# A two-layer block with a product-key expert layer: key stage in whole slabs, a shorter key search, and another order on ScalarE

## The chip, the core and the metric

The kernel runs on one core of one Trainium2 chip, in one launch. The metric is the device time of an execution in microseconds (us); lower is better. The core has TensorE (PE, with its weight loads as PEld), VectorE (DVE), ScalarE (ACT), GpSimd (POOL) and SyncE (SP), and 16 DMA engines that all its queues share.

## The reference, cut to what matters

Both layers end in the same expert layer, and it takes about three quarters of the time. It has 16,384 experts of 2048 numbers each, in two tables `u` and `v` (128 MB each). For each of 256 tokens and 8 heads it takes the 16 best of 128 scores in each of two halves, the 16 best of the 256 sums of those, and the experts that they name:

```python
sc = jnp.einsum('bshtd,htkd->bshtk', q, subkeys)
top_s, top_i = lax.top_k(sc, 16)
cand = top_s[..., 0, :, None] + top_s[..., 1, None, :]
best_s, best_c = lax.top_k(cand.reshape(b, s, 8, 256), 16)
i1 = take_along_axis(top_i[..., 0, :], best_c // 16)
i2 = take_along_axis(top_i[..., 1, :], best_c % 16)
idx = i1 * 128 + i2;  gate = softmax(best_s)
hid = einsum('td,tkd->tk', x, u[idx])
out = einsum('tk,tkd->td', gelu(hid) * gate, v[idx])
```

## The kernel before

**Two ways to the same rows.** For 192 of the 256 tokens (`ND`) the kernel multiplies with all experts: `u` is read as 128 slabs of 128 experts (1 MB each), and gates, zero nearly everywhere, pick the chosen ones. For the first 64 tokens (`NS`) it gathers the chosen rows: 64 gathers a layer (`PAIRS`, 1 MB each, 128 rows), each followed by a dot of the 128 rows with the tokens' x. The gathers stand on GpSimd's queue and land in two buffers (`SLOTS`); gather n+2 waits for dot n.

**A slab of `u`.** SyncE's queue loads the slab into `raw` (three buffers, `RAW_SLABS`). A slab has two halves of 128 x 1024 (pieces); a ring of four (`RING`) holds their rounded-up part `wh`, made by ScalarE (`hi`, L597), and their rest in half precision, `halves`, made by VectorE (`lo`, L1743), which needs `wh` and frees `raw`. TensorE (`slab_u`, L1073) does for each half eight high products (`ps <- xx,wh`, 384 columns: the sum of the high part of x and the side sum with its low part) and eight side products (`ps <- halves`, 192 columns); all matmuls share L1043. ScalarE copies the side sums of a slab to `cross` (`take_side`, L637); after the first half of the next slab TensorE adds them by a product with the identity (`fold`); then ScalarE takes the result out through gelu (`gelu`, L777), to `arena` in the key stage or `hring` in the spread stage, from where SyncE stores it.

**Order.** Each engine runs what is written out for it; semaphores join them. ScalarE's order in each slab stands in `trip`: side sums, high half, gelu, high half. VectorE's order is a table: `UNIT_FILL` says how many low halves (`L`) and dots (`D`) stand in each of seven gaps of a unit of the search.

**The stages of the expert layer.** The key stage is slabs 0 to 63, in trips of four. Beside it VectorE searches in 16 units (8 heads, two blocks of 128 tokens): `max` finds eight values, `max_index` their places, `match_replace` takes them out; two halves of 128 scores, then 256 sums, then compares and sums that look the indices up (L1973 to L1993). The tail of a unit is decoded within the next unit. Unit 8 ends with the row indices (`idx_f`), which TensorE spreads over partitions ahead of slab 20 (`REP_TRIP` 5), and then the gathers can start. After unit 16 come softmax and selection, and TensorE turns them ahead of slab 64. The spread stage is slabs 64 to 127, in eight trips of eight. In each, six groups (`Q_PIECE`) of four tokens get their dense gates: VectorE compares (`compare`, L2051, two instructions), ScalarE scales eight rows (`gate_rows`, L792, to `hot_w`), TensorE multiplies them, ScalarE copies the gates out (`gates_out`, L783), VectorE multiplies the kept slabs (`gate_kept`, L2043). Here dots stand after the halves of `DOT_PIECE`, 46 in eight trips. Then `v` is multiplied (the V stage), in which the rows of `v` are gathered too.

## Time and profile before

| what | value |
|---|---|
| median of 3 runs | 3280.0 us (3279.31 to 3281.93) |
| profiled execution: its own time | 3274.78 us |
| its span, mean granted clock | 3273.0 us, 0.996 |
| busy share: PE, PEld, DVE, ACT, POOL | 98%, 84%, 85%, 61%, 12% |
| moved by DMA | 969 MB, mean 296 GB/s |

| stage | layer 0 | layer 1 |
|---|---|---|
| key stage, slabs 0 to 63 | 511 to 811 us | 2056 to 2356 us |
| spread stage, slabs 64 to 127 | 811 to 1131 us | 2356 to 2675 us |
| PE, DVE, ACT busy in the key stage | 287.4, 289.2, 173.6 us | 286.0, 288.5, 173.1 us |
| PE, DVE, ACT busy in the spread stage | 309.3, 298.2, 283.9 us | 310.3, 298.7, 284.4 us |

Busy shares are means over stages; the stages are read apart. A slab is told by its fold, a matmul from `cross` that occurs once a slab. A timeline row gives start, duration, operation and count of instructions put together, and in brackets what the engine waited for just before. A wait is put down to what came last.

### The profile page before, as it was taken

To read this page: it belongs to the slowest core of one execution; us is meant where nothing else is said; L and a number is where in the kernel's file an instruction comes from. 1 tells how busy PE (TensorE), PEld (TensorE's weight loads), DVE (VectorE), ACT (ScalarE), POOL (GpSimd) and SP (SyncE) were. 2 spreads that over 40 slices of the span, in tenths; PEclk is the share of its full clock that TensorE was granted. 3 is DMA by queue.
4 is the path that set the end of the run, shared out by engine and by line. 5 is a ranking of instruction groups with operands and counts; after the bars stand their busy time and mean duration, and the time that the engine had idled before them with its cause. 6 is when DMAs were issued, how large, how long until landed. Compare 5 with 4: busy or idle time off the path is not lost. (4 is left out here: it accounts for less than half of the span.)

```text
span 3273.0 us, 52190 instructions
## 1 busy us (share of the span) xinstructions
PE 3196.3 (98%) x19468; PEld 2762.0 (84%) x19468; DVE 2773.5 (85%) x4026; ACT 1997.0 (61%) x3631; POOL 406.6 (12%) x266
## 2 busy tenths in 40 slices
PE   9999999999999999999999999999999999999998
PEld 8888888889888888888888887888888888888887
DVE  5775669999999888888887756999999988888887
ACT  4444556556898755555555545655688875555555
POOL 0000000011111122222100000001111112222220
PEclk9999999999999999999999999999999999999999
DMA  7553345698999989999984344578899999999995
GB/s 273 183 183 140 116 161 192 257 342 339 379 379 378 373 335 372 362 371 367 365 305 156 117 152 158 197 278 338 335 390 380 373 369 366 368 370 368 363 368 224
DMA packets 169221, 969.07 MB, mean 296 GB/s; under 512 B 18912, under 2 KB 52704, under 8 KB 55648
## 3 DMA queue, kind: packets, MB, share of 16 engines
q1 hardware_dynamic: 132192, 698.61, 56.2%
q0 software_dynamic: 36864, 268.45, 22.3%
q8 instruction: 80, 1.31, 0.1%
q14 instruction: 85, 0.70, 0.1%
HBM read 951.26 MB, written 15.73 MB: 295 GB/s over the span
## 5 line engine op out<-in xcount | busy, mean ns | idle before, releaser
L597 ACT ACTIVATE wh<-raw 128x1024 fp32r<-128x1024 f32 x1264 | 1335.5, 1060 | 833.5 <-PE ps L1043 663.9
L1043 PE MATMUL ps<-xx,wh 128*128 128x384 f32 (+1 forms) x5504 | 1333.7, 358 | 6.8 <-DVE xx L1755 4.0
L1043 PE MATMUL ps<-wh,act 128*128 128x512 f32 x3584 | 1190.6, 390 | 0.4 <-issue 0.2
L1746 DVE TENSOR_TENSOR wl<-raw,wh 128x1024 fp32r<-128x1024 f32 x752 | 905.9, 1221 | 323.8 <-ACT wh L597 322.2
L1043 PEld LDWEIGHTS ps<-xx,wh 128*128 128x128 f32 x5504 | 955.5, 189 | 73.5 <-issue 5.7
L1043 PE MATMUL ps<-wl,act 128*128 128x512 f32 x2304 | 897.6, 390 | 0.0
L1043 PEld LDWEIGHTS ps<-wh,act 128*128 128x128 f32 x3584 | 673.8, 188 | 142.0 <-DVE wl L1746 1.0
L1743 DVE SCALAR_TENSOR_TENSOR halves<-raw,wh 128x1024 f16<-128x1024 f32 x512 | 615.2, 1213 | 63.5 <-ACT wh L597 63.1
L1043 PEld LDWEIGHTS ps<-wl,act 128*128 128x128 f32 x2304 | 433.2, 188 | 89.7
L1043 PE MATMUL ps<-halves 128*128 128x192 f16 x4096 | 428.3, 248 | 22.5 <-DVE halves L1743 20.6
L1043 PEld LDWEIGHTS ps<-halves 128*128 128x128 f16 x4096 | 312.7, 98 | 112.4 <-issue 62.8
L1043 PE MATMUL ps<-xx,wl 128*128 128x256 f32 x1408 | 393.9, 280 | 0.0
L1711 POOL DMA_INDIRECT arena<-in_urows,idx x128 | 150.9, 1179 | 1907.3 <-DVE idx L2018 1072.0
L1711 POOL DMA_INDIRECT arena<-in_v,idx x128 | 246.8, 1928 | 839.4 <-DVE arena L2126 818.4
L2126 DVE SCALAR_TENSOR_TENSOR arena<-arena,hid 128x2048 f32<-128x2048 f32 x128 | 300.2, 2345 | 2.2 <-DMA arena<-in_v,idx 2.1
L1928 DVE SCALAR_TENSOR_TENSOR arena<-arena 128x2048 f32<-128x2048 f32 x128 | 292.0, 2281 | 0.0
L1043 PEld LDWEIGHTS ps<-xx,wl 128*128 128x128 f32 x1408 | 266.2, 189 | 0.5
L792 ACT ACTIVATE hot_w<-hot,x_space 128x128 f16<-128x128 f16 x768 | 242.1, 410 | 8.0 <-DVE hot L2051 8.0
L637 ACT ACTIVATE cross<-ps 128x192 fp32r<-128x192 f32 (+1 forms) x272 | 89.8, 330 | 124.5 <-PE ps L1043 122.2
L1043 PE MATMUL ps<-cross,ident_r 128*128 128x192 f32 (+1 forms) x272 | 92.0, 338 | 16.9 <-ACT cross L637 15.7
L777 ACT ACTIVATE arena<-ps 128x192 f32<-128x192 f32 x128 | 42.1, 329 | 108.3 <-PE ps L1043 108.2
L1043 PE MATMUL ps<-arena 64*128 64x128 f32 (+9 forms) x712 | 93.3, 317 | 7.5 <-DVE arena L2004 4.6
(225 smaller groups left out, 1751.2 us busy)
## 6 DMA issues: line engine op xcount, KB each, us to landing
raw<-in_u SPq DMA_DIRECT2D x256, 1024.0 KB, 7.1
raw<-in_v SPq DMA_DIRECT2D x256, 1024.0 KB, 7.4
raw<-in_w SPq DMA_DIRECT2D x118, 1024.0 KB, 4.8
h_scratch<-hring SPq DMA_DIRECT2D x128, 96.0 KB, 7.3
hring<-h_scratch SPq DMA_DIRECT2D x128, 96.0 KB, 7.1
arena<-in_memT SPq DMA_DIRECT2D x4, 512.0 KB, 7.2
raw<-in_w SPq DMA_DIRECT2D x4, 512.0 KB, 7.8
arena<-in_xT SPq DMA_DIRECT2D x4, 512.0 KB, 8.5
```

The source lines that it names most:

```text
L597: nc.scalar.activation(wh[:, j, :], raw_piece(p), ACT.Copy, scale=W_UP if scaled_up(p) else 1.0)\
L637: nc.scalar.activation(cross[:, 0:n], ps[:, bank, n:2 * n], ACT.Copy).then_inc(cross_out, 1)
L777: nc.scalar.activation(h_kept[:, k, :] if kept else hring[:, j, :], ps[:, j, 0:ND], ACT.Gelu, scale=W_DOWN).then_inc(evac_done, 1)
L792: nc.scalar.activation(hot_w[:, q % 2, w, t, :], one_hot(q, 0, t), ACT.Copy, scale=gate_hl[w][:, of // NS, of % NS:of % NS + 1]).then_inc( ...
L1043: return nc.tensor.matmul(out, lhs, rhs, start=start, stop=stop, **kw)
L1711: pool.indirect_dma_start(out=gbuf[n % SLOTS], out_offset=None, in_=rows_of, in_offset=bass.IndirectOffsetOnAxis(ap=idx[:, j:j + 1], axis=0))\
L1743: v.scalar_tensor_tensor(out=wl16[:, j, :], in0=raw_piece(p), scalar=W_UP, in1=wh[:, j, :].bitcast(F32), op0=ALU.mult, op1=ALU.subtract).t ...
L1746: v.tensor_tensor(wl[:, j, :], raw_piece(p), wh[:, j, :].bitcast(F32), ALU.subtract).then_inc(lo_ready, 1)
L1928: v.scalar_tensor_tensor(out=rows_u, in0=rows_u, scalar=1.0, in1=xrep, op0=ALU.mult, op1=ALU.mult, accum_out=hid[:, j:j + 1]).then_inc(slo ...
L2126: v.scalar_tensor_tensor(out=vacc, in0=rows_v, scalar=hid[:, j:j + 1], in1=vacc, op0=ALU.mult, op1=ALU.add).then_inc(slot_free, 1)
```

## The change

- **TensorE.** `slab_u` does a slab in one go: 16 high products (the fold of the slab before after the tenth, `FOLD_AT`), then 16 side products. It waits for both high halves, then for both low halves.
- **High and low halves.** One instruction makes both halves of a slab (`hi_slab`, `low_slab`, 128 x 2048). On ScalarE the order in a slab becomes side sums, high halves, gelu, and in the spread stage gates out and gate rows.
- **Search.** Two units run interleaved, in eight steps; each works on its scores in place (no copy), and on 112 sums and not 256: the first 4 of one half with all 16, the other 12 with the first 4. Decoding is done for four units at once (`batch`, nine steps) in half precision, the steps standing between those of the next pair.
- **Placing.** The search ends by slab 42 (`EXP_SLAB`), the row indices are spread ahead of slab 12, the selection is turned ahead of slab 48 (`SEL_TRIP` 12). Ten dots stand in the last pairs and the last batch, and then one after each low slab up to slab 63 (22 and four around the softmax); the spread stage has four a trip, after every second slab.
- **Gates.** `compare` is one instruction for both one-hot halves; its constant `iota_h` moves from x's free space to free space in `halves`, and is set up at slab 51. The 16 chunks of x in half precision lie in four parts of five (`XS`).

Cut to its core (removed lines that the kernel above shows are left out):

```diff
+XS = 5
...
-REP_TRIP = 5
+REP_TRIP, SEL_TRIP = 3, 12
...
+FOLD_AT = 9
...
-UNIT_FILL = ([("L", "", "L", "", "L", "L", "")] * 2 + [("L", "L", "L", "", "L", "L", "")]
-             + [("L", "L", "L", "L", "L", "L", "")] * 7 + [("LL", "LL", "LL", "LL", "LDL", "LL", "DL")]
-             + [("LDLL", "", "LDLL", "L", "LDLL", "L", "L")] * 4 + [("LDLL", "", "LLL", "L", "LDLL", "L", "L")])
-UNIT_TAIL = ("L", "LD", "L", "L", "L", "", "")
-SPARED = (2, 5)
+PAIR_FILL = ([("L", "", "L", "", "L", "", "L", "")] * 3
+             + [("S", "S", "", "S", "S", "", "S", "S"), ("S", "S", "S", "S", "S", "", "S", "S"),
+                ("S", "S", "D", "S", "S", "SD", "S", "S"), ("S", "S", "SD", "S", "S", "SD", "S", "S"),
+                ("S", "S", "D", "S", "S", "SD", "S", "S")])
+LAST_FILL = ("S", "D", "S", "D", "S", "D", "S", "D", "S")
+BATCH = 4
+KEY_PAIRS = 4 * TOPK + (TOPK - 4) * 4
+EXP_SLAB, SETUP_SLAB, REST_DOTS = 42, 51, 22
+DOT_SLABS = (1, 3, 5, 7)
...
+    iota_h = halves[:, RING - 1, PC + ND:PC + ND + 4 * P]
...
+        def hi_slab(p):
+
+            act.wait_ge(piece_used, p - (RING - 1))
+            act.wait_ge(lo_ready, p - 2)
+            n, j = p // 2, p % RING
+            act.wait_ge(raw_full[n % RAW_SLABS], 16 * (n // RAW_SLABS + 1))
+            nc.scalar.activation(wh[:, j:j + 2, :], raw[:, n % RAW_SLABS, :].rearrange("p (e c) -> p e c", e=2), ACT.Copy,
+                                 scale=W_UP if scaled_up(p) else 1.0).then_inc(hi_ready, 2)
...
-                    ahead = [2 * s + 2, 2 * s + 3]
                     take_side(u0, i * slabs + (s - 1), (s - 1) % 2, ND)
-                    for n in ahead[:-1]:
-                        hi(i * (2 * slabs) + (u0 + n), n % RING)
                     if first and s == 1:
                         scores_out(layer, PEER_H - 1)
+                    hi_slab(u0 + 2 * (i * slabs + s + 1))
                     gelu(i * slabs + (s - 1), s - 1)
-                    for n in ahead[-1:]:
-                        hi(i * (2 * slabs) + (u0 + n), n % RING)
                     for k in range(Q_TRIP) if spread else ():
...
+            for i in range(1, SEL_TRIP):
+                trip(i, BODY, exp_at=EXP_SLAB % BODY if i == EXP_SLAB // BODY else None)
...
+            j = 2 * s4 % RING
+
+            def part(w, kc):
+                return w[:, j + kc // (KC // 2), kc % (KC // 2) * P:(kc % (KC // 2) + 1) * P]
+
+            pe.wait_ge(hi_ready, piece + 2)
+            for kc in range(KC):
+                last = mm(both, part(wh, kc), xx[:, kc, :, NS:], kc == 0, False, skip_group_check=True)
+                if kc == FOLD_AT and side_of is not None:
                     fold(side_of, 1 - par_, side_t0)
-                if then is not None:
-                    then(e)
+            last.then_inc(piece_used, 1)
+            if then is not None:
+                then(0)
+            pe.wait_ge(lo_ready, piece + 2)
+            for kc in range(KC):
+                if x_from is not None and kc % XS == 0:
+                    pe.wait_ge(x16_ready, x_from + kc // XS + 1)
+                last = mm(side, part(wl16, kc), x16[:, kc // XS, kc % XS, :], False, kc == KC - 1, skip_group_check=True)
+            last.then_inc(piece_used, 1)
+            if then is not None:
+                then(1)
...
+            def low_slab():
+                n = next(at_slab)
+                p = u0 + 2 * n
+                j = p % RING
+                dve.wait_ge(hi_ready, p + 2)
+                dve.wait_ge(piece_used, p - 2)
+                v.scalar_tensor_tensor(out=wl16[:, j:j + 2, :],
+                                       in0=raw[:, p // 2 % RAW_SLABS, :].rearrange("p (e c) -> p e c", e=2), scalar=W_UP,
+                                       in1=wh[:, j:j + 2, :].bitcast(F32), op0=ALU.mult, op1=ALU.subtract)\
+                    .then_inc(lo_ready, 2)
...
+            def unit(i, step):
+                keys, b = sc[:, i, :, :], i % 2
+                tv, ti, rest = top_v[:, b, :, :], top_i[:, b, :, :], s1[:, b, :, :]
+                sums, left = cand[:, b, 0, :], cand[:, b, 1, :]
+                values = sel[:, 2, i * TOPK:(i + 1) * TOPK]
+                found = best_i[:, i // BATCH % 2, 0, i % BATCH * TOPK:(i % BATCH + 1) * TOPK]
+                if step == 0:
+                    if i < PEER_H:
+                        dve.wait_ge(sc_evac, PEER_H * layer + i + 1)
+                else:
+                    own.upto(marked[i])
+                if step == 0:
+                    for t in range(2):
+                        own.mark(v.max(tv[:, t, 0:8], keys[:, t, :]))
+                elif step == 1:
+                    for t in range(2):
+                        own.mark(v.max_index(ti[:, t, 0:8], tv[:, t, 0:8], keys[:, t, :]))
+                        own.mark(v.match_replace(out=rest[:, t, :], in_to_replace=tv[:, t, 0:8],
+                                                 in_values=keys[:, t, :], imm_value=NEG))
+                elif step == 2:
+                    for t in range(2):
+                        own.mark(v.max(tv[:, t, 8:16], rest[:, t, :]))
+                elif step == 3:
+                    own.mark(v.tensor_tensor(sums[:, 0:4 * TOPK].rearrange("p (a b) -> p a b", a=4),
+                                             tv[:, 0, 0:4].unsqueeze(2).broadcast_to([P, 4, TOPK]),
+                                             tv[:, 1, :].unsqueeze(1).broadcast_to([P, 4, TOPK]), ALU.add))
+                    own.mark(v.tensor_tensor(sums[:, 4 * TOPK:].rearrange("p (a b) -> p a b", b=4),
+                                             tv[:, 0, 4:TOPK].unsqueeze(2).broadcast_to([P, TOPK - 4, 4]),
+                                             tv[:, 1, 0:4].unsqueeze(1).broadcast_to([P, TOPK - 4, 4]), ALU.add))
+                    for t in range(2):
+                        own.mark(v.max_index(ti[:, t, 8:16], tv[:, t, 8:16], rest[:, t, :]))
+                elif step == 4:
+                    own.mark(v.max(values[:, 0:8], sums))
+                    own.mark(v.tensor_copy(top_f[:, i // BATCH % 2, :, :, i % BATCH], ti))
+                elif step == 5:
+                    own.mark(v.max_index(found[:, 0:8], values[:, 0:8], sums))
+                    own.mark(v.match_replace(out=left, in_to_replace=values[:, 0:8], in_values=sums, imm_value=NEG))
+                elif step == 6:
+                    own.mark(v.max(values[:, 8:16], left))
+                else:
+                    own.mark(v.max_index(found[:, 8:16], values[:, 8:16], left))
+                marked[i] = own.n
+            def batch(b, step):
+                at, row, col = (best_i[:, b % 2, k, :] for k in range(3))
+                whole, by16, by4 = (place[:, k] for k in range(3))
+                r1, r2 = rank[:, 0], rank[:, 1]
+                tall, least = row_at[:, 0], row_at[:, 1]
+                own.upto(marked["batch"] if step else max(marked[i] for i in range(b * BATCH, (b + 1) * BATCH)))
+                if step == 0:
+                    own.mark(v.tensor_scalar(row, at, 4, None, ALU.logical_shift_right))
+                    own.mark(v.tensor_scalar(col, at, 2, None, ALU.logical_shift_right))
+                elif step == 1:
+                    own.mark(v.tensor_copy(place, best_i[:, b % 2].rearrange("p w (u k) -> p w k u", u=BATCH)))
...
+                elif step == 6:
+                    own.mark(v.tensor_tensor(pick.rearrange("p w k a u -> p (w k) a u"),
+                                             rank.rearrange("p w k u -> p (w k) u").unsqueeze(2)
+                                             .broadcast_to([P, 2 * TOPK, TOPK, BATCH]),
+                                             iota_u.unsqueeze(1).broadcast_to([P, 2 * TOPK, TOPK, BATCH]), ALU.is_equal))
+                elif step == 7:
+                    flat = pick.rearrange("p w k a u -> p w k (a u)")
+                    own.mark(v.tensor_tensor(flat, flat, top_f[:, b % 2].rearrange("p w a u -> p w (a u)").unsqueeze(2)
+                                             .broadcast_to([P, 2, TOPK, TOPK * BATCH]), ALU.mult))
+                else:
+                    for w in range(2):
+                        own.mark(v.tensor_reduce(
+                            sel[:, w, b * BATCH * TOPK:(b + 1) * BATCH * TOPK].rearrange("p (u k) -> p k u", u=BATCH),
+                            pick[:, w].rearrange("p k a u -> p k u a"), AX.X, ALU.add))
+                marked["batch"] = own.n
...
+            for p in range(UNITS // 2):
+                tail = itertools.count() if p and p % 2 == 0 else None
+                for n in range(8):
+                    for i in (2 * p, 2 * p + 1):
+                        unit(i, n)
+                        if tail is not None:
+                            step = next(tail)
+                            if step < 9:
+                                batch(p // 2 - 1, step)
+                            elif p == PEER_H // 2 and step == 10:
+                                own.upto(marked["batch"])
+                                v.scalar_tensor_tensor(out=idx_f, in0=sel[:, 0, 0:P], scalar=float(KEYS),
+                                                       in1=sel[:, 1, 0:P], op0=ALU.mult, op1=ALU.add).then_inc(sidx_ready, 1)
+                    fill(PAIR_FILL[p][n])
...
+            for n in range(9):
+                batch(UNITS // BATCH - 1, n)
+                fill(LAST_FILL[n])
...
+            for n in range(EXP_SLAB + 4, KEPT):
...
+                fill("SD")
...
+                v.tensor_tensor(hot[:, q % 2, :, :].rearrange("p w (j t) -> p w j t", t=4),
+                                iota_h.rearrange("p (j t) -> p j t", t=4).unsqueeze(1).broadcast_to([P, 2, P, 4]),
+                                sel_t[:, :, 4 * q:4 * q + 4].unsqueeze(2).broadcast_to([P, 2, P, 4]),
+                                ALU.is_equal).then_inc(onehot_ready, 2)
...
+                for n in range(WIDE):
+                    q = i * Q_TRIP + COMPARE_SLAB.index(n) if n in COMPARE_SLAB else None
+                    if q is not None:
+                        compare(q)
+                    low_slab()
+                    if q is not None and q >= 3:
+                        gate_kept(q - 3)
+                    if n in DOT_SLABS:
+                        dot()
```

VectorE where the low halves go over from the query weights (`wl`) to `u` (`halves`), layer 0. The names are buffers: `arena` holds all of the search, `raw` a slab as loaded, `wh` its high halves, `wl` and `halves` low halves. Before:

```order
L1983 TENSOR_TENSOR arena<-arena 128x512
L1986 TENSOR_TENSOR arena<-arena 128x256
L1989 MAX_INDEX arena<-arena 128x8 x2
L1746 TENSOR_TENSOR wl<-raw,wh 128x1024
L1993 TENSOR_REDUCE arena<-arena 128x2x16
L1995 MAX arena<-arena 128x8
L1746 TENSOR_TENSOR wl<-raw,wh 128x1024
L1999 CAST arena<-arena 128x32
L2000 MAX_INDEX arena<-arena 128x8
L2001 MATCH_REPLACE arena<-arena 128x256
L2007 MAX arena<-arena 128x8
```

and now:

```order
L2030 TENSOR_SCALAR arena<-arena 128x64
L1991 MAX arena<-arena 128x8 x2
L2032 CAST arena<-arena 128x192
L1768 SCALAR_TENSOR_TENSOR halves<-raw,wh 128x1024
L1994 MAX_INDEX arena<-arena 128x8
L1995 MATCH_REPLACE arena<-arena 128x128
L1994 MAX_INDEX arena<-arena 128x8
L1995 MATCH_REPLACE arena<-arena 128x128
L2034 SCALAR_TENSOR_TENSOR arena<-arena 128x64
L1994 MAX_INDEX arena<-arena 128x8
L1995 MATCH_REPLACE arena<-arena 128x128
```

What stood as one unit's steps with low halves between has become steps of two units and of a batch, in which a low half stands after several searches.

VectorE around the softmax over the selection. Before:

```order
L1928 SCALAR_TENSOR_TENSOR arena,hid<-arena 128x2048
L2027 TENSOR_REDUCE arena<-arena 128x16
L1743 SCALAR_TENSOR_TENSOR halves<-raw,wh 128x1024
L2031 TENSOR_SCALAR arena<-arena 128x16
L2032 RECIPROCAL arena<-arena 128x16
L1743 SCALAR_TENSOR_TENSOR halves<-raw,wh 128x1024
L2035 TENSOR_TENSOR arena<-arena 128x256
L1743 SCALAR_TENSOR_TENSOR halves<-raw,wh 128x1024 x2
L2063 CAST x_space<-iota 128x4x128
```

and now:

```order
L2087 COPY arena<-arena 128x16
L2088 TENSOR_TENSOR arena<-arena 128x256
L1945 SCALAR_TENSOR_TENSOR halves<-raw,wh 128x2x1024
L1963 SCALAR_TENSOR_TENSOR arena,hid<-arena 128x2048
L1945 SCALAR_TENSOR_TENSOR halves<-raw,wh 128x2x1024
L1963 SCALAR_TENSOR_TENSOR arena,hid<-arena 128x2048
L2092 TENSOR_REDUCE arena<-arena 128x16
L1945 SCALAR_TENSOR_TENSOR halves<-raw,wh 128x2x1024
L1963 SCALAR_TENSOR_TENSOR arena,hid<-arena 128x2048
L2095 TENSOR_SCALAR arena<-arena 128x16
```

Each whole slab (128x2x1024) is now followed by a dot (to `hid`), where low halves stood with one dot in eight.

ScalarE in the spread stage (`cross` side sums, `hring` gelu out, `hot_w` gate rows). Before:

```order
L597 ACTIVATE wh<-raw 128x1024
L777 ACTIVATE hring<-ps 128x192
L597 ACTIVATE wh<-raw 128x1024
L783 ACTIVATE arena<-ps 128x64x4
L637 ACTIVATE cross<-ps 128x192
L597 ACTIVATE wh<-raw 128x1024
L777 ACTIVATE hring<-ps 128x192
L597 ACTIVATE wh<-raw 128x1024
L783 ACTIVATE arena<-ps 128x64x4
L792 ACTIVATE hot_w<-hot,x_space 128x128 x8
L637 ACTIVATE cross<-ps 128x192
```

and now:

```order
L624 ACTIVATE wh<-raw 128x2048
L800 ACTIVATE hring<-ps 128x192
L806 ACTIVATE arena<-ps 128x64x4
L815 ACTIVATE hot_w<-hot,x_space 128x128 x8
L660 ACTIVATE cross<-ps 128x192
L624 ACTIVATE wh<-raw 128x2048
L800 ACTIVATE hring<-ps 128x192
L806 ACTIVATE arena<-ps 128x64x4
L660 ACTIVATE cross<-ps 128x192
L624 ACTIVATE wh<-raw 128x2048
L800 ACTIVATE hring<-ps 128x192
```

The second high half has moved ahead of the gelu, into one instruction with the first.

## Rows read from the trace of the kernel before

**Rows 1.** Stage windows; from:to, us, then busy (x instructions), PEclk, DMA share, GB/s
```profile
511.00:811.00 300.00, 287.42 (x2200) 262.35 (x2200) 289.21 (x651) 173.60 (x268) 31.93 (x20) 0.99 0.78 290
811.00:1131.00 320.00, 309.33 (x2511) 281.25 (x2509) 298.18 (x368) 283.93 (x691) 47.03 (x47) 1.00 0.97 379
1150.00:1700.00 550.00, 550.00 (x2427) 455.05 (x2426) 479.27 (x491) 307.94 (x486) 122.54 (x62) 1.00 0.94 359
...
980.00:990.00 10.00, 10.00 (x87) 9.28 (x85) 8.51 (x10) 9.70 (x25) 0.94 (x1) 1.00 1.02 418
```

**Rows 2.** TensorE timeline, layer 0; start us, us, engine line op, operands [idle before]
```profile
512.05 1.68 PE L1043 MATMUL ps<-xx,wh 128*128 128x384 f32 x8
...
690.21 0.34 PE L1043 MATMUL ps<-cross,ident_r 128*128 128x192 f32 x1
...
804.12 0.34 PE L1043 MATMUL ps<-cross,ident_r 128*128 128x192 f32 x1
804.29 1.58 PE L1043 MATMUL ps<-xx,wh 128*128 128x384 f32 x8
805.71 0.83 PE L1043 MATMUL ps<-halves 128*128 128x192 f16 x8
...
807.81 0.83 PE L1043 MATMUL ps<-halves 128*128 128x192 f16 x8
808.43 0.34 PE L1043 MATMUL ps<-cross,ident_r 128*128 128x192 f32 x1
...
811.49 1.64 PE L1043 MATMUL ps<-xx,wh 128*128 128x384 f32 x8
...
1130.12 0.36 PE L1043 MATMUL ps<-cross,ident_r 128*128 128x192 f32 x1 [0.26 <-ACT cross L637]
```

**Rows 3.** Waits, first 511 to 811 us, then 811 to 1131: us in total, times, longest
```profile
PE ps L1043 <- DVE halves L1743: 9.4, 14, 1.1
...
ACT wh L597 <- DMA raw<-in_u: 15.4, 17, 3.2
...
PE ps L1043 <- ACT cross L637: 8.5, 14, 1.5
```

**Rows 4.** TensorE timeline where the row indices are first needed
```profile
609.00 0.49 PE L1043 MATMUL ps<-arena 128*128 128x128 f32 x2 [2.29 <-DVE arena L2004]
609.29 2.85 PE L1043 MATMUL ps<-xx,wh 128*128 128x384 f32 x8
```

**Rows 5.** VectorE timeline over one unit of the search with its fills
```profile
738.42 0.29 DVE L1949 COPY arena<-arena 128x256 f32<-128x256 f32 x1
...
740.16 2.29 DVE L1928 SCALAR_TENSOR_TENSOR arena<-arena 128x2048 f32<-128x2048 f32 x1
...
742.37 2.36 DVE L1743 SCALAR_TENSOR_TENSOR halves<-raw,wh 128x1024 f16<-128x1024 f32 x2
...
765.93 0.29 DVE L1949 COPY arena<-arena 128x256 f32<-128x256 f32 x1
```

**Rows 6.** VectorE groups by form, 500 to 1130 us: x count | busy us, mean ns
```profile
L2051 DVE TENSOR_TENSOR hot<-x_space,sel_t 128x512 f16<-128x512 f16 x96 | 37.9, 434 | 0.0
...
L1973 DVE TENSOR_TENSOR arena<-arena,iota 128x512 f32<-128x512 f32 x15 | 10.3, 684 | 0.0
...
L1967 DVE FIND_INDEX8 arena<-arena 128x8 uint32<-128x128 f32 x28 | 8.0, 285 | 0.0
```

**Rows 7.** ScalarE timeline: the scores of head 5 go to SBUF
```profile
506.86 0.59 ACT L757 ACTIVATE arena<-ps 128x512 f32<-128x512 f32 x1
```

**Rows 8.** DMA issues, 660 to 800 us: count, median us from issue to landing
```profile
arena<-in_urows,idx POOLq DMA_INDIRECT x15, 8.2
```

**Rows 9.** ScalarE timeline in the spread stage: one half, gates out, eight gate rows
```profile
1092.49 1.05 ACT L597 ACTIVATE wh<-raw 128x1024 fp32r<-128x1024 f32 x1
1093.44 0.37 ACT L783 ACTIVATE arena<-ps 128x256 f32<-128x256 f32 x1
1093.70 2.52 ACT L792 ACTIVATE hot_w<-hot,x_space 128x128 f16<-128x128 f16 x8
```

204 lines of the change are left out of this document (68 added, 136 removed).

## The prediction

> **What bounds the kernel now.** I read the busy times by stage first [rows 1]. Two stages of each layer are touched: the first 64 slabs of the expert product (called the key stage here, 511 to 811 us) and the last 64 (the spread stage, 811 to 1131 us); layer 1 repeats both within 1 us in length. In the key stage TensorE is busy 287 of 300 us and VectorE 289: two engines near full. In the spread stage TensorE has 309 of 320, VectorE 298, ScalarE 284, and the DMA engines a share of 0.97 at 379 GB/s. In the V product TensorE is busy throughout, so nothing can be won there. Next, TensorE's own rows [rows 2]: from fold to fold an unhindered slab takes 808.43 - 804.12 = 4.31 us. Sixty-four of them are 276 us, while slab 0 starts at 512.05 and slab 64 at 811.49, 299.4 us later [rows 2]. The waits [rows 3] say who is late: VectorE's low halves in the key stage (9.4 us), the side sums copied by ScalarE in the spread stage (8.5 us), besides one wait of 2.29 us for the row indices [rows 4]. Behind that one the next eight matmuls took 2.85 us against 1.57 to 1.58 us elsewhere [rows 2, 4]: TensorE had idled and ran a while at 1.2 GHz, worth some 1.7 us with its side products; layer 1 shows the same wait without that slowdown. So the gain to be had is VectorE time, ScalarE order and bytes, and I follow TensorE's path through three stretches of layer 0.
>
> **Part 1: slabs 0 to 36.** VectorE's search cost now: from one unit's first instruction (738.42) to the next (765.93) are 27.5 us [rows 5]. In it are 12 low halves and 3 dots. A dot holds the engine 742.37 - 740.16 = 2.21 us, a low half about 1.13 (2.36 for two less the overlap) [rows 5], together 20.2, so a unit costs 7.3 us, 117 for 16. After the change a unit sheds its copy, sums 112 candidates and not 256, and does its index decoding in batches of four. By the kinds' durations (a search of 128 elements 285 ns [rows 6], the others by their length) I count 4.1 us for a unit (two maxima 0.5, four searches of 128 1.05, two maxima 0.4, sums 0.25, two searches 0.55, and 1.3 in the second round at half length). A batch compares and multiplies 2048 half-precision elements and reduces twice 1024. 512 such elements took 434 ns, against 684 ns in fp32 [rows 6], which puts 2048 at 1.2 us if the broadcast keeps that speed and 2.2 if not; I take 1.2, since the row before has the same inner four. The reduce I price at the fp32 rate, 2.3 in all. A batch is then 5.5 us, and the search 16 x 4.1 + 4 x 5.5 = 88 us (bounds 85 to 96), some 29 less. A low half of a whole slab should take about a dot's time, 2.2 for 2.26.
>
> Where does it go? The search is packed into 42 slabs instead of 60, and three places come late. (a) The units' pairs wait for the scores of the later one. ScalarE writes those of head 5 at 506.86 [rows 7]; pair 2 then needs 8.2 us of search, batch 0 (5.5, newly here) and four low halves (4.5), so the last half of slab 1 is done near 524.4 and TensorE ends slab 1 at 525.7, where two unhindered slabs from 512.05 on would end at 520.7 [rows 2]: 5.0 lost, some 3.6 of it new. (b) The indices come after low halves 8 to 12, batch 1 and unit 8's sixth step, at about 576. TensorE is at slab 12 by 572: it loses 4.5 us, against 2.5 now, and one slow spell (1.7) as now. (c) Pair 6 has 8.2 + 5.5 + 8 x 2.2 + 2 x 2.21 = 35.7 us for 8 slabs, 1.3 above TensorE's 34.4; with its uneven batch steps 1.9 lost. All other stretches give VectorE 3.6 to 4.2 us a slab, and it can be late by 3.0 us, the length of the 16 high products that now stand first.
>
> TensorE's slab itself gets shorter. It changes from fp32 to half-precision products and back twice a slab now, once afterwards. Eight high products behind the fold take 805.71 - 804.29 = 1.42 us; behind side products they take 2.10 less 0.62, 1.48 [rows 2], so a change back costs some 0.06. One of two goes, and the fold then stands among products of its own kind: I take 0.05 (0 to 0.1), a slab of 4.25. Sum: slab 37 starts at 525.7 + 8.5 + 3.8 (turning x, unchanged) + 34.0 + 4.5 + 25 x 4.25 + 1.9 + 1.7 = 686.4. Now it starts 2.1 us before the fold of 690.21 [rows 2], at 688.1. **Part 1: -1.7** (bounds -6 to +5).
>
> **Part 2: slabs 37 to 63.** Here 26 dots stand one behind each slab's low half, where now there are about one for two slabs. VectorE would need 2.2 + 2.21 = 4.4 us a slab, only just too much. But each slab then moves 1.05 MB of weights and 1.05 MB of gathered rows. The spread stage moves 379 GB/s at a share of 0.97 [rows 1]: nearly full. 2.10 MB at that rate are 5.5 us, at 418, a best ten-microsecond stretch [rows 1], 5.0. The gathers say the same. Two buffers: gather n+2 starts when dot n ends, and lands 8.2 us later [rows 8]; with the dot itself a pair of slabs takes at least 8.2 + 0.3 + 2.2 = 10.7, so 5.4 a slab. I take 5.4. The first gathers lie ready, so 24 intervals count: 24 x 5.4 + 4.5 = 134, from the first dot 5.2 us into the stretch; full weight buffers and VectorE's 3.0 us give back 6; one more slab follows: 134 + 5.2 - 6 + 4.7 = 137.9. The six turns of the selection (now between slabs 63 and 64) hide in it. Now the stretch takes 811.49 - 688.1 = 123.4. **Part 2: +14.5** (7 with a cycle of 5.1, 21 with 5.65).
> The Trainium skill ("DMA: Bandwidth & Descriptors", Specifications) gives a core about 358 GB/s from HBM. The row's 379 is above that, so the trace disagrees. By 358 the cycle would be an estimated 5.86 us and the stretch 11 longer a layer.
>
> **Part 3: the spread stage.** Eight slabs with six gate groups are a round. Now eight rounds take 1130.12 - 811.49 = 318.6 us [rows 2], 39.8 each; without waits it would be 8 x 4.31 + 6 x 0.5 = 37.4. Two causes. First a loop on ScalarE: fold, copy-out, second high half, gates out, eight gate rows, side copy, fold. A half takes 0.95, gates out 0.26, the rows 2.52 less the overlap of 0.1 [rows 9], and with 0.36 for the fold, 0.22 for the copy-out and 0.3 for the side sums the loop is 4.5 us, above a slab's 4.31. The change puts both halves ahead of the copy-out, so this loop loses 0.95. Second, weights that land late: ScalarE waits 15.4 us for them [rows 3] at a DMA share of 0.97. Dots fall from 5.75 to 4 a round: (12 x 1.05 + 0.8) MB in 37 us are 362 GB/s, the V stage's load (359, share 0.94), where TensorE is never kept waiting [rows 1]. ScalarE's own work is 8 x 2.29 + 6 x (0.26 + 2.42) = 34.4 us a round [rows 9], counting 1.87 for a whole slab's high half, and fits beside TensorE's 8 x 4.25 + 6 x 0.48 = 36.9, but with 2.5 us to spare only; within three slabs with gates it falls 0.9 behind, and the fold gives it 1.6. So I add 0.6 a round for late weights: 37.5, 300 in all. VectorE needs 32.5 a round. **Part 3: -18** (-22 to -6).
>
> Layer 0: -1.7 + 14.5 - 18 = -5. Layer 1 has no slow spell, and its stretches are otherwise within 1.5 us of these (the table of stages): -5 again. The profiled execution took 3274.8 us (span 3273.0 and 1.8 around it), 5.2 below the median of 3280.0; I carry the difference over: 3270.
>
> **The rivals.** *ScalarE becomes the bound of the spread stage (slower).* If late weights hit it for over 2.5 us a round, each us more is TensorE's. For: it has 93% to do, waits 2 us a round today, and everything stands in one order behind a high half that is now twice as long. Against: fewer bytes. With today's 2 us a round straight on TensorE's 36.9, rounds of 39.0 give 7 and not 18 a layer: 3292. *The run of dots is not held by bytes.* Then VectorE sets 4.4 a slab, part 2 takes 121 and saves 2: 3270 - 34 = 3236. For: gathers never made a dot wait yet; against: [rows 1, 8]. *The lower HBM rate,* worked as this kernel's mechanism: if gathers and weights together get a tenth less than the mixed traffic now, the cycle is 5.85, +11 a layer: 3292; the skill's figure above would make it so.
>
> **How the numbers follow.** My case has 0.63, its own range 3256 to 3284. ScalarE 0.17, no byte limit 0.12, lower rate 0.08. Below 3273.4 (0.2%, about what a measurement can tell from no change) lie six tenths of my case and the second rival: 0.50. Above 3286.6 lie the other two and a little of mine: 0.27. Between them 0.23. The range 3250 to 3296 leaves out the second rival and the far ends of the others.
>
> **What would show it.** Right: fold to fold 4.25 in calm slabs; a wait of 4 us in slab 1 and at the indices; from slab 38 to 63 dots 5.2 to 5.6 us apart, VectorE waiting for gathers and DMA share 1.0; the spread stage near 300 us with hardly a wait for side sums. Wrong: dots 4.4 apart, or ScalarE over 95% busy in the spread stage with folds waiting, or a low half of a slab that costs more than 2.3 us.

## The result, and the profile after

The changed kernel takes a median of 3311.95 us (3306.2 to 3312.97, four runs) against 3279.65 (3277.07 to 3281.93, four runs): a ratio of 1.0095, with a 95% interval of 1.0078 to 1.0113. It is slower by about 1%, where 3270 us was predicted and a range of 3250 to 3296. The profiled execution took 3306.2 us against 3274.78, its span 3304.0 against 3273.0.

Where the 31.0 us of span come from, by the folds (the product that closes a slab, one in each):

| stretch, fold to fold | layer 0: before, after | layer 1: before, after |
|---|---|---|
| slab 0 to 36 | 170.3, 174.2 | 169.7, 171.8 |
| slab 36 to 63 | 123.4, 155.9 | 124.3, 155.4 |
| slab 63 to 127 | 316.5, 299.5 | 315.2, 298.6 |

That is +19.4 and +16.6 us. From the last fold of layer 0 to the first of layer 1 the changed kernel is 5.1 us shorter, which the prediction has as nothing. Spread stage: -17 us a layer, as predicted (-18). First part: +3.9 and +2.1 where -1.7 was predicted. The run of dots: +32.5 and +31.1 where +14.5 was predicted, and this decides.

These are the stages of layer 0 in the windows view of the changed kernel (columns as in [rows 1]): the first slabs, the start of the run of dots, the rest of it, the spread stage.

```profile
512.00:694.00 182.00, 172.69 (x1316) 164.26 (x1315) 158.66 (x398) 95.16 (x123) 9.50 (x8) 0.96 0.71 259
694.00:760.00 66.00, 58.08 (x414) 54.67 (x412) 55.71 (x48) 33.50 (x44) 21.45 (x11) 0.95 0.90 339
760.00:850.00 90.00, 68.21 (x487) 63.67 (x488) 67.84 (x49) 34.66 (x44) 38.26 (x15) 0.96 0.87 342
850.00:1150.00 300.00, 297.30 (x2491) 285.62 (x2490) 260.85 (x228) 274.67 (x623) 50.67 (x34) 1.00 0.96 361
```

From 760 to 850 us TensorE is busy 68.2 of 90 us and VectorE 67.8: neither is the bound. GpSimd, which only issues gathers there, is busy 38.3 us, 2.6 a gather. And the DMA engines have a share of 0.87 at 342 GB/s, below the 0.97 and 379 of [rows 1]. The waits view of 694 to 850 us of the changed kernel names the chain (us in total, times, longest):

```profile
DVE arena L1963 <- DMA arena<-in_urows,idx: 32.4, 18, 3.1
...
PE ps L1063 <- DVE halves L1945: 29.6, 16, 3.1
```

VectorE waits for gathers in its dots, TensorE for the low half that stands behind each dot. One period of it, in the timeline of GpSimd and VectorE of the changed kernel:

```profile
806.84 2.29 DVE L1963 SCALAR_TENSOR_TENSOR arena<-arena 128x2048 f32<-128x2048 f32 x1 [1.57 <-DMA arena<-in_urows,idx]
809.05 0.08 DVE L1963 DVE_READ_ACCUMULATOR arena<-arena 128x1 f32 x1
809.05 2.29 DVE L1945 SCALAR_TENSOR_TENSOR halves<-raw,wh 128x2048 f16<-128x2048 f32 x1
809.41 2.74 POOL L1736 DMA_INDIRECT arena<-in_urows,idx  x1 [3.33 <-DVE arena L1963]
812.53 2.29 DVE L1963 SCALAR_TENSOR_TENSOR arena<-arena 128x2048 f32<-128x2048 f32 x1 [1.19 <-DMA arena<-in_urows,idx]
...
818.69 2.29 DVE L1963 SCALAR_TENSOR_TENSOR arena<-arena 128x2048 f32<-128x2048 f32 x1 [1.65 <-DMA arena<-in_urows,idx]
```

The dot that began at 806.84 frees its buffer; the gather into it is issued at 809.41 and its data are used at 818.69, 9.3 us later, by the next dot but one. Two dots thus take 11.85 us: 5.9 a slab. Fifteen intervals from 757.25 to 847.77 have a mean of 6.0. The issue itself takes 2.74 us. Where it begins as the low half begins, and behind another instruction, it takes 0.94 (same kernel and view):

```profile
741.90 0.42 DVE L2099 TENSOR_TENSOR arena<-arena 128x256 f32<-128x256 f32 x1
742.23 2.33 DVE L1945 SCALAR_TENSOR_TENSOR halves<-raw,wh 128x2048 f16<-128x2048 f32 x1
742.25 0.94 POOL L1736 DMA_INDIRECT arena<-in_urows,idx  x1 [5.20 <-DVE arena L1963]
```

Of the 17 issues from 747 to 846 us, 16 began within a low half (L1945), took 2.43 to 2.75 us and ended 0.8 us behind it; that is the pattern of a lock which VectorE holds for an instruction. In the kernel before a low half has half the length (the 2.35 us below are two of them), and such issues took 1.68 us:

```profile
731.64 2.35 DVE L1743 SCALAR_TENSOR_TENSOR halves<-raw,wh 128x1024 f16<-128x1024 f32 x2
731.99 1.68 POOL L1711 DMA_INDIRECT arena<-in_urows,idx  x1 [7.52 <-DVE arena L1928]
```

VectorE waited for gathers alone from 693 to 850 us, 32.4 us in 18 waits, and never for TensorE.

### The profile page after: what moved, and what is told of

Read it like the earlier page. It is cut to its first block, busy times and chain, and to the rows that moved or that the text cites. A ratio compares the mean times of both kernels' runs of the same rounds, so it can differ in the third digit from the quotient of the medians.

```text
span 3304.0 us, 51665 instructions
## 1 busy us (share of the span) xinstructions
PE 3190.4 (97%) x19468; PEld 2807.7 (85%) x19468; DVE 2691.8 (81%) x3546; ACT 1958.8 (59%) x3377; POOL 483.1 (15%) x266
## 4 chain that ended last, share of the span: by engine, by line
PE 81%; DVE 7%; DMA 7%; ACT 2%; issue 2%; SPq 0%; ACTq 0%; DVEq 0%
PE ps L1063 81%; DMA arena<-in_urows,idx 5%; DVE halves L1945 2%; DMA raw<-in_w 1%; DVE arena L1963 1%; ACT wh L624 1%; DVE wl L1771 1%; DVE arena L2054 1%; DVE xx L1780 0%; DMA arena<-in_v,idx 0%; DMA raw<-in_v 0%; DVE arena L2187 0%; DVE halves L1768 0%; ACT arena L693 0%; ACT wh L610 0%
## 5 line engine op out<-in xcount | busy, mean ns | idle before, releaser
L610 ACT ACTIVATE wh<-raw 128x1024 fp32r<-128x1024 f32 x756 | 798.7, 1062 | 771.8 <-PE ps L1063 653.4
L1063 PEld LDWEIGHTS ps<-xx,wh 128*128 128x128 f32 x5504 | 973.1, 191 | 72.9 <-issue 6.1
L1945 DVE SCALAR_TENSOR_TENSOR halves<-raw,wh 128x2048 f16<-128x2048 f32 x252 | 576.9, 2289 | 118.3 <-issue 105.8
L1736 POOL DMA_INDIRECT arena<-in_urows,idx x128 | 227.8, 1779 | 1851.3 <-DVE idx L2080 1004.7
L624 ACT ACTIVATE wh<-raw 128x2048 fp32r<-128x2048 f32 x254 | 486.2, 1914 | 13.0 <-DMA raw<-in_u 9.9
L1063 PE MATMUL ps<-halves 128*128 128x192 f16 x4096 | 388.4, 249 | 75.0 <-DVE halves L1945 66.7
L1063 PEld LDWEIGHTS ps<-halves 128*128 128x128 f16 x4096 | 332.3, 99 | 115.8 <-DVE halves L1945 82.2
L1063 PEld LDWEIGHTS ps<-arena 128*64 128x64 f32 (+4 forms) x712 | 62.4, 162 | 34.1 <-issue 16.5
```

The lines of the kernel that those rows point to most:

```text
L610: nc.scalar.activation(wh[:, j, :], raw_piece(p), ACT.Copy, scale=W_UP if scaled_up(p) else 1.0)\
L624: nc.scalar.activation(wh[:, j:j + 2, :], raw[:, n % RAW_SLABS, :].rearrange("p (e c) -> p e c", e=2), ACT.Copy, scale=W_UP if scaled_up(p ...
L1063: return nc.tensor.matmul(out, lhs, rhs, start=start, stop=stop, **kw)
L1736: pool.indirect_dma_start(out=gbuf[n % SLOTS], out_offset=None, in_=rows_of, in_offset=bass.IndirectOffsetOnAxis(ap=idx[:, j:j + 1], axis=0))\
L1945: v.scalar_tensor_tensor(out=wl16[:, j:j + 2, :], in0=raw[:, p // 2 % RAW_SLABS, :].rearrange("p (e c) -> p e c", e=2), scalar=W_UP, in1=w ...
```

## The experiments

All stretches are read from fold to fold, as in the table above; a pair of numbers is layer 0 and layer 1.

**Is it the lock?** Edit of e1_gap:

```diff
                         dot()
+                        if gap:
+                            ...
+                            own.mark(v.tensor_reduce(gap_out, xrep[:, 0:384].rearrange("p (a b) -> p a b", a=24),
+                                                     AX.X, ALU.add))
```

> The changed kernel with a small reduce (128x384) on VectorE behind each of the 26 dots of slabs 42 to 63, ahead of the next low half; its result is used by nobody. Theory lock: in the changed kernel's trace the issue of a gather on GpSimd takes 2.75 us where it begins while a whole-slab low half runs on VectorE, and ends 0.8 us after it, but 0.94 us where a reduce or cast runs. So the issue should fall to 0.94, a pair of slabs lose 1.8 us, the dots stand 5.0 to 5.2 us apart and not 5.9, slabs 37 to 63 take about 140 us and not 156, and the whole about 3280 us. Theory bytes (that of the prediction, with its rate set too high): the issue gets shorter, but the gathers land as late as now since 2.1 MB a slab are moving anyway; dots stay 5.8 to 5.9 apart and the time within 4 us of 3312.

Measured: 3295.74 us (ratio to before 1.0043, 1.0027 to 1.006), 16 less than the changed kernel. The edit reaches 22 dots a layer and not 26: `REST_DOTS` is 22 with the four around the softmax in it, and the other four of the 26 that the prediction counts stand in the last batch. Of the 22 issues in layer 0, 19 fell to 0.94 us; three began after the reduce, within the next low half, and took 2.89. One of the 19, in the timeline of e1_gap:

```profile
777.36 0.55 DVE L1977 TENSOR_REDUCE arena<-arena 128x24 f32<-128x384 f32 x1
777.71 0.95 POOL L1737 DMA_INDIRECT arena<-in_urows,idx  x1 [6.06 <-DVE arena L1964]
777.82 2.28 DVE L1946 SCALAR_TENSOR_TENSOR halves<-raw,wh 128x2048 f16<-128x2048 f32 x1
```

So the lock is real, and half of the theory holds: the stretch from slab 36 to 63 fell from 155.9 and 155.4 to 151.1 and 152.9 in the profiled execution (which at 3303.56 was the slowest of its four, and whose spread stage in layer 0 took 305.0), not to 140. From the issue's begin to the dot that waited for it a median gather still took 9.6 us (22 waited for from slab 42 on, both layers; 9.3 in the changed kernel). Windows of 725 to 850 us, the changed kernel and e1_gap:

```profile
725.00:850.00 125.00, 99.77 (x710) 93.22 (x709) 95.11 (x71) 51.98 (x68) 50.51 (x21) 0.96 0.88 344
```

```profile
725.00:850.00 125.00, 102.24 (x734) 95.50 (x731) 105.36 (x92) 54.85 (x71) 25.57 (x21) 0.96 0.94 360
```

GpSimd's time halves, the DMA share rises from 0.88 to 0.94, the rate from 344 to 360 GB/s: with the issue out of the way, the engines that move the data look like the next limit, which the next experiment asks.

**Bytes or the latency of a gather?** Edit of e5_half_raw, on e1_gap:

```diff
             for k in range(S_EXP):
-                slab(u_in[row0 + k, :, :], u0 + 2 * k)
+                if 48 <= k < 63:
+                    ...
+                    sp.dma_start(raw[:, n % RAW_SLABS, 0:PC], u_in[row0 + k, :, 0:PC]).then_inc(...)
+                else:
+                    slab(u_in[row0 + k, :, :], u0 + 2 * k)
```

> The kernel of e1_gap (issues of 0.94 us) in which the weights of slabs 48 to 62 are loaded only in their first half, so that these slabs move 1.57 MB and not 2.10; the second halves of raw keep old data, and so the product of these slabs is not the real one. Theory bytes: at the 357 to 360 GB/s that e1_gap moved there, 1.57 MB take 4.4 us, so the dots stand 4.4 to 4.8 us apart (VectorE's own work is 2.2 + 2.2 + 0.5 = 4.9 and becomes the bound), and a gather lands sooner than 9.5 us after its issue begins. Slabs 36 to 63 take 137 to 141 us and not 151. Theory latency (two buffers and a gather that takes as long whatever else moves): the gather still takes 9.4 us, the dots stay 5.6 to 5.9 apart and the stretch stays at 149 to 153.

Measured: slabs 36 to 63 in 144.0 and 145.3 us, a gather in 8.3 us (median of the 19 waited for), the window of 725 to 850 us at a share of 0.86:

```profile
725.00:850.00 125.00, 102.91 (x759) 95.78 (x759) 113.86 (x98) 58.85 (x84) 26.88 (x22) 0.99 0.86 315
```

Neither theory alone. A quarter fewer bytes in 15 slabs take 1.3 us off a gather and 7 us off the stretch; the remaining 8.3 us with two buffers still allow no more than a dot in (8.3 + 0.35 + 2.2) / 2 = 5.4 us. The loop through two buffers is what bounds the run; other traffic and the blocked issue set its length. What share of the 8.3 us is a gather's own time was not tried.

**Fewer dots in the run.** Edit of e2_even5:

```diff
-EXP_SLAB, SETUP_SLAB, REST_DOTS = 42, 51, 22
-DOT_SLABS = (1, 3, 5, 7)
+EXP_SLAB, SETUP_SLAB = 42, 51
+DOT_SLABS = (0, 2, 3, 5, 6)
+RUN_DOTS = (47, 49, 51, 53, 55, 57, 59, 61, 63, 46)
+REST_DOTS = 4 + len(RUN_DOTS)
...
-                fill("SD")
+                fill("SD" if n in RUN_DOTS else "S")
```

> The changed kernel with dots placed otherwise: five a trip of eight slabs in the spread stage (40 and not 32), and from slab 42 to 63 only 14 and not 22, one behind every second slab from slab 46 on. If the run of dots is the loss, whatever makes it slow, slabs 37 to 63 come to 128 to 134 us and not 156; the spread stage moves 14.5 MB a round and at 379 to 400 GB/s stays at 37.4 to 38.5 us a round. Whole: 3255 to 3270 us. Rival (the spread stage gained its 17 us a layer by fewer bytes alone): its rounds go back towards 39.8 at five dots, half of the gain is lost, and the whole is 3270 to 3285.

Measured: 3263.32 us (ratio 0.9949, 0.9931 to 0.9966). Slabs 36 to 63 take 131.4 and 131.9 us, the spread stage 299.7 and 299.6: five dots a trip cost nothing there. The placing of the dots alone is worth 49 us of median and turns the loss into a gain.

**Six a trip.** e7_even6 has `DOT_SLABS = (0, 1, 2, 4, 5, 6)` and 6 dots from slab 42 to 63.

> The changed kernel with six dots a trip in the spread stage (48 dots; the kernel before had 46) and six in slabs 42 to 63. Five a trip cost nothing in e2_even5 at 384 GB/s and a share of 0.98. Six would be 15.5 MB in 37.4 us, 414 GB/s, as much as the best ten microseconds of any trace. Theory bytes: the rounds grow to 38.3 to 39.5 us, the spread stage to 306 to 316 us. Rival order (ScalarE's order alone made the stage slow before): it stays at 299 to 302. Slabs 36 to 63 fall to 124 to 129.

Measured: the key stage as expected (126.9 and 125.8 us), but the spread stage 343.0 and 333.5 us, far beyond either theory; 3323.48 us (one execution). Waits of 870 to 1130 us in e7_even6:

```profile
PE ps L1065 <- ACT cross L662: 25.5, 15, 4.0
ACT hot_w L817 <- DVE hot L2127: 23.6, 8, 4.7
DVE arena L1965 <- DMA arena<-in_urows,idx: 21.9, 12, 2.9
```

Read upwards, one reading of these waits is: a dot waits for its gather, the compare behind it on VectorE comes late, ScalarE stands at the gate rows that need it, and the side sums queued behind those hold TensorE. Three dots in three slabs (0, 1, 2 and 4, 5, 6) want a third gather before two buffers can give it. The edit set both the number and the bunching, and which of them costs more was not tried; the kernel before had 5.75 a trip, spread apart, at 316 us.

**What the spread stage gained from.** Three edits of the kernel before, and one of the changed kernel. e6_before_order moves `gelu` behind the second `hi`; e10_before_dots4 has `DOT_PIECE = (2, 7, 10, 15)` with the other 14 dots in `UNIT_FILL` and `UNIT_TAIL`; e11_before_dots4_order has both.

> The kernel before with ScalarE's new order alone: side sums, first high half, second high half, gelu, all other parts as before (5.75 dots a round, half slabs). Theory order: the loop through fold, gelu, second high half, gates out, gate rows and side sums (4.5 us) loses 0.95 us and no longer sets the pace; the spread stage falls from 316 us to 304 to 309, the rest of the gain of the changed kernel being the fold in the middle of one run of high products and fewer dots. Rival: late weights set the pace; then it stays within 3 us of 316.

> The kernel before with four dots a trip in the spread stage and not 5.75; the other 14 stand in its key stage, which may get longer. All else as before (half slabs, its ScalarE order). Theory dots (gathered bytes and their latency made the spread stage slow before): it falls from 316 us to 299 to 303. Rival slab (whole-slab order on TensorE and shorter compares make it): it stays at 312 to 317. Theory sum of the prediction (the ScalarE loop and late weights about half each): 305 to 311.

> The kernel of e10_before_dots4 with ScalarE's new order as well (both high halves ahead of gelu). If late weights hid the gain of the order in e6_before_order (316 to 316), it appears now: 5 to 10 us less in the spread stage than in e10_before_dots4. Rival: the order alone is worth nothing with half slabs, within 2 us of e10_before_dots4.

| kernel | spread stage, us | whole, one execution |
|---|---|---|
| before | 316.5, 315.2 | 3274.8 |
| e6_before_order | 318.0, 314.6 | 3281.1 |
| e10_before_dots4 | 305.7, 305.0 | 3334.1 (longer key stage) |
| e11_before_dots4_order | 298.0, 298.0 | 3315.3 (the same) |
| changed | 299.5, 298.6 | 3306.2 |

Order alone gives nothing, four dots alone 10.5 us, and order on top of four dots another 7.4: together the whole gain, without any whole slab. The waits of 870 to 1130 us say why; first e6_before_order, then e10_before_dots4, then e11_before_dots4_order:

```profile
ACT wh L597 <- DMA raw<-in_u: 17.1, 15, 2.7
...
PE ps L1043 <- ACT hring L777: 5.6, 4, 2.9
```

```profile
DVE halves L1743 <- ACT wh L597: 28.7, 27, 1.7
ACT hring L777 <- PE ps L1043: 19.8, 14, 1.4
...
PEld ps L1043 <- ACT cross L637: 4.2, 14, 0.3
...
ACT cross L637 <- PE ps L1043: 2.2, 13, 0.2
```

```profile
ACT cross L637 <- PE ps L1043: 9.2, 13, 0.7
ACT hring L777 <- PE ps L1043: 6.5, 14, 0.5
```

With 5.75 dots ScalarE waits 17.1 us for weights (14.6 in the kernel before, same window), and in the new order the gelu stands behind that wait too (a new wait of 5.6 us), so what the order saves is lost again. With four dots that wait is gone from the list, ScalarE's loop is left (19.8 us of waiting for the fold), and the order takes 13 us of that away, of which 7 come back as a longer wait for the side sums (9.2 us, 2.2 in e10_before_dots4).

e4_gelu_first turns the order in the changed kernel round:

```diff
-                    hi_slab(u0 + 2 * (i * slabs + s + 1))
                     gelu(i * slabs + (s - 1), s - 1)
+                    hi_slab(u0 + 2 * (i * slabs + s + 1))
```

> The changed kernel with ScalarE's order in a slab as side sums, gelu, high halves, so that the high halves stand behind the fold again. Theory order: the loop fold, gelu, high halves, gates out, gate rows, side sums is then 5.4 us against a slab of 4.77 with gates, and the spread stage grows from 299.5 us by 20 to 30 us a layer. Rival: the stage's gain came from fewer dots and their bytes; then the stage stays within 3 us of 299.5.

Measured: 335.1 and 333.0 us in the spread stage, 3394.11 in all. Theory order holds, with a size above its 20 to 30 us. Waits of 870 to 1130 us:

```profile
ACT hring L800 <- PE ps L1063: 41.0, 50, 2.0
...
PE ps L1063 <- ACT cross L660: 18.2, 37, 0.8
```

In this kernel the high halves of a whole slab must stand ahead of the gelu: the other order costs 35 us a layer.

**The first slabs.** Edit of e3_batch_late:

```diff
-                tail = itertools.count() if p and p % 2 == 0 else None
+                late = {3: 0, 4: 1, 6: 2}
+                tail = itertools.count() if p in late else None
...
-                                batch(p // 2 - 1, step)
+                                batch(late[p], step)
```

> The changed kernel with the first batch of decoding (5.2 us of VectorE) beside the fourth pair of units and not beside the third. Theory: TensorE's wait of 4.0 us in slab 1 goes, and with it 2.7 us of products at the lower clock behind it; slabs 0 to 36 are 6 to 7 us shorter in each layer, and the whole profiled execution some 12 us shorter. Rival: VectorE's path to the row indices is what counts; then the wait at slab 12 grows by what slab 1 gives back, and the time stays.

Measured: slabs 0 to 36 in 167.4 and 166.0 us (174.2 and 171.8), all of it from slab 1, in a single execution of 3296.16 us, and the time at the indices unchanged. The rival is out. Slab 1 in the changed kernel, TensorE's timeline:

```profile
525.43 2.74 PE L1063 MATMUL ps<-halves 128*128 128x192 f16 x16 [4.00 <-DVE halves L1768]
527.88 3.48 PE L1063 MATMUL ps<-xx,wh 128*128 128x384 f32 x10
...
532.38 1.49 PE L1063 MATMUL ps<-halves 128*128 128x192 f16 x16
```

and in e3_batch_late:

```profile
521.27 1.49 PE L1063 MATMUL ps<-halves 128*128 128x192 f16 x16
522.55 1.99 PE L1063 MATMUL ps<-xx,wh 128*128 128x384 f32 x10
```

The wait of 4.00 us is followed by products at 1.2 GHz (granted clock 0.50 from 525.5 to 531 us): 2.74 for 1.49 and 3.48 for 1.99 us, 2.7 us more.

**Mends together.** e8_best has e2_even5, e3_batch_late, `REP_TRIP` 4, and the decoding of the indices within the sixth pair. e9_best2 places its early dots anew (2, 1 and 3 in the last three pairs, 2 in `LAST_FILL`, 3 around the softmax, 13 in slabs 46 to 63), and e12_best_gap adds the reduces of e1_gap.

> Three mends on the changed kernel together: the dots of e2_even5 (40 in the spread stage, 14 in slabs 42 to 63), the late first batch of e3_batch_late, and the row indices spread ahead of slab 16 and not 12 (VectorE decodes them within the sixth pair). Expected: 25 us a layer from the first, 6.3 from the second, and from the third the wait at slab 12 with its slow products, 5.6 us a layer; no wait at slab 16. Slabs 0 to 36 take 161 to 163 us, the whole 3311.95 - 50 - 12.6 - 11 = 3238 to 3244 us. Rival: the indices come no earlier for VectorE and the gathers start 17 us later, so that the early dots wait and push slabs 20 to 30; then 3248 to 3255.

Measured: 3262.64 us (ratio 0.9929, 0.9905 to 0.9952). No wait at slab 12, but slabs 0 to 36 take 170.9 and 170.6. The cause that its rival names is there, with a size above the rival's 3255 us: the first dot stands close behind the indices, and TensorE then waits up to 7.4 us. VectorE in e8_best:

```profile
588.88 0.23 DVE L2083 TENSOR_SCALAR idx<-ps 64x64 uint32<-64x64 f32 x1
589.14 0.87 DVE L2001 MAX8 arena<-arena 128x8 f32<-128x128 f32 x4
597.12 2.29 DVE L1965 SCALAR_TENSOR_TENSOR arena<-arena 128x2048 f32<-128x2048 f32 x1 [7.12 <-DMA arena<-in_urows,idx]
```

> The kernel of e8_best with the early dots placed anew: in e8_best the first dot stood one gap behind the decoding of the indices and VectorE waited 7.1 us for its gather (8.0 us from issue), which held TensorE up by 7.4 us with 2.4 us of slow products behind. Now the first dot stands five gaps behind; the sixth, seventh and eighth pairs have 2, 1 and 3 dots, the last batch 2, the softmax part 3, slabs 46 to 63 have 13 of 18, and the spread stage 40 as in e8_best. Expected: slabs 0 to 36 in 159 to 162 us (170.9 in e8_best), slabs 36 to 63 in 124 to 130, the whole 3262.6 - 2 x 12 = 3236 to 3246 us. Rival (gathers can't come faster than one in 5.9 us, so 13 dots in 18 slabs of 4.3 us, one in 5.9, tip over): slabs 46 to 63 lose 5 to 10 us a layer and the whole is 3248 to 3258.

Measured: 3237.66 us (ratio 0.9869, 0.9849 to 0.9889). Slabs 0 to 36 take 159.8 and 161.0 us. But slabs 36 to 63 take 133.2 and 132.8: its rival held there, and the total came out in the forecast all the same.

> The kernel of e9_best2 with the small reduce of e1_gap behind its 16 dots from slab 42 on. In e9_best2 most of these gathers still took 2.4 to 2.8 us to issue, and one landed 11.5 us after its issue began and held TensorE up for 4.8 us. Theory lock: issues of 0.94 us let each gather start 1.8 us sooner, e1_gap was worth 16 us of median with 26 dots a layer, so 16 dots give about 8 to 10 us: 3228 to 3232 us, slabs 36 to 63 some 4 us shorter in each layer. Theory bytes: the gathers land as late as before, and the reduces cost 0.5 us each of a VectorE that has room; within 3 us of 3237.7.

Measured: 3227.55 us (ratio 0.9849, 0.9823 to 0.9875), 1.5% below the kernel before, and 10 us below e9_best2 by the medians, 7 by the two ratios. Slabs 36 to 63 take 123.8 and 129.8 us, 9.4 and 3.0 less. Windows of 690 to 815 us, e9_best2 and then e12_best_gap:

```profile
690.00:815.00 125.00, 113.62 (x840) 107.66 (x839) 103.42 (x76) 64.89 (x86) 37.68 (x18) 0.96 0.93 357
```

```profile
690.00:815.00 125.00, 119.24 (x907) 113.64 (x906) 114.31 (x94) 70.76 (x100) 21.04 (x18) 0.99 0.97 380
```

Here the shorter issue counts as its theory had it: with room in the gather loop, an issue 1.8 us shorter lets the same engines move 380 GB/s and not 357, and TensorE is busy 5.6 us more in this window.

## Why the prediction was wrong

**Part 2 failed, by one term.** The mechanism was right: the run of dots is bound by the loop through two gather buffers, VectorE waits for gathers and TensorE for the low halves. The cycle was put at 5.4 us, and over the last fifteen intervals it is 6.0. The prediction gives its 24 intervals 134 us (24 x 5.4, and 4.5 of which it does not say what for); they took 149.5 us (698.24 to 847.77) and 150.2 in layer 1, which is 15 and 16 us of the 18 and 17 us missing. The 8.2 us of [rows 8] came from a stretch in which dots stood 8 to 11 us apart and the engines moved 341 GB/s; here it is 9.3. Two things set it: an issue behind a low half of double length (2.74 against 1.68 us), which the change itself made, and the traffic beside it (e5_half_raw: 1.3 us for a quarter of the bytes). How they share the 1.1 us between 8.2 and 9.3 is not shown: the issue alone is longer by as much, but with short issues and 360 GB/s e1_gap is no lower, at 9.6. The prediction took a whole-slab low half as neutral because VectorE's own time is the same, 2.29 us against two of 1.21, and never asked who waits for that instruction's end. The Trainium skill ("SBUF — State Buffer", Who interferes with whom) says that VectorE and GpSimd share a port pair, that a VectorE instruction with two SBUF inputs contends with a GpSimd instruction that reads SBUF, and that the later one blocks until the first ends. The trace agrees where VectorE is first (2.74 against 0.94 us), and adds that the issue of an indirect gather is such a GpSimd instruction. Where the issue is first it shows no block: in e1_gap the low half at 777.82 took 2.28 us while the issue ran from 777.71 to 778.66. Half-precision compares, which also read two inputs, hold an issue up too: 1.68 us for those that begin within one of 1.22 us, 1.15 within one of 0.69. The prediction had no term for this.

The other 1 to 3 us are at the ends of the run, where the prediction let full weight buffers and VectorE's slack give back 6 us. TensorE's clock has no part in it, though it looks so: in the stretch of layer 0 TensorE is busy 126.2 us, against 118.7 in the kernel before for as many products, mostly since four of its waits are followed by products at 1.2 GHz (granted clock 0.57 to 0.61 over the 4 us behind each). But VectorE sets the time there and never waits for TensorE, and behind each of these spells TensorE waits for a low half again, so what a spell lost came off the next wait.

**The rate.** As it turned out, the run moved 344 GB/s, 9% less than the 379 taken from [rows 1], which is the condition of the rival "lower rate" (3292 us, a chance of 0.08). Its condition came true and its cause did not: e12_best_gap moves 380 GB/s with dots and weights mixed, above the 358 of the Trainium skill ("DMA: Bandwidth & Descriptors", Specifications). The rate was low since the loop left the DMA engines idle, a share of 0.88 there against 0.97.

**Part 1.** The three late places were named, and their waits are there. Slab 1: 6.8 us more than in the kernel before, 4.0 of it waiting and 2.7 slow products behind it, which were not in the sum. The prediction has 5.0 there, but only 3.6 of it new: it counts from 520.7, two slabs of 4.3 us, where the kernel before is at 522.11, since slab 0 takes 5.7 us (eight other products and a wait of 0.39 us stand in it):

```profile
517.78 1.66 PE L1043 MATMUL ps<-xx,wh 128*128 128x384 f32 x8
...
522.11 1.64 PE L1043 MATMUL ps<-xx,wh 128*128 128x384 f32 x8
```

So slab 1 is 3.2 us of the 5.6 missing in layer 0. The indices: 3.4 us of wait, and 3.2 for their two products and slow ones behind, 6.6 against 6.2. Pair 6: 2.2 against 1.9. A calm slab takes 4.29 us and not 4.25, 1.4 us over the stretch: the change of product type that goes is worth 0.02, not 0.05. Together that is 5.3 of the 5.6. The unit costs held: 1.22 us for a compare of 2048 in half precision (1.2), 2.34 for the two reduces (2.3), 2.29 for a low half.

**Part 3 was right in size and, by the last experiments, in cause.** 299.5 and 298.6 us against 300. The two causes were said to be ScalarE's loop and late weights; e11_before_dots4_order and e10_before_dots4, one execution each, give them 7.4 and 10.5 us. What was not foreseen is that they do not add: the order is worth nothing while weights are late. The rival "ScalarE becomes the bound" is out: it is busy 274.7 of 300 us, and TensorE waits 2.7.

**The 5.1 us between the layers** stay open: nothing was tried there. The kernel before has a wait of 1.8 us and slow products at that place in layer 0; the changed kernel's trace shows neither.

## What to carry to other kernels

When a resource is refilled through n buffers, price a run by the loop (issue, landing, use, release) over n, at the traffic of the run itself, and keep demands spaced by at least that; the same 64 dots cost 49 us more bunched than spread. When an instruction is made longer, ask what other engine can start only at its end: here a small reduce that blocks nothing, put ahead of it, was worth 7 to 10 us. And count the products at 1.2 GHz that may stand behind a longer wait of TensorE (2.7 us behind one of 4.0), but only where TensorE sets the time: in the run of dots the next wait took them up.

## What the runs showed of the hardware

- The issue of a gather on GpSimd takes 0.94 us beside a maximum, a reduce or a cast of VectorE, 1.15 when it begins within a half-precision compare of 0.69 us, 1.68 within one of 1.22 us, and until 0.8 us after the end of a low half if it begins within one (2.74, in the half-slab kernel 1.68). If it begins 0.02 us after the low half does, and behind another instruction (742.25 against 742.23), it is not held up.
- One change less between fp32 and half-precision products in a slab of TensorE, with the fold among products of its own kind, is worth 0.02 us (4.31 to 4.29), not 0.05.
- Behind the wait of 4.0 us in slab 1 the granted clock was 0.50. From slab 36 to 63 of layer 0 in the changed kernel TensorE ran at 1.2 GHz for a while behind its waits of 2.1 (at 738 us), 2.7, 2.9 and 3.1 us, and stayed at 2.4 GHz behind those of 2.1 (at 847 us) and 2.5 us and all ten between 0.5 and 1.9.
